# First products of seven stages by 512 columns, and five reorderings of read-outs and splits, in a two-block fp32 transformer kernel

## What is computed

```python
def first_block(x, mem, ...):
    for l in range(DEPTH):                       # DEPTH = 2, x is [1, 256, 1024]
        y = swiglu(rms_norm(x, ffn1_pre_g[l]), gate[l], up[l], down[l])   # 1024 -> 2816 -> 1024
        x = x + 0.5 * rms_norm(y, ffn1_post_g[l])
        y = hybrid_mixer(rms_norm(x, mix_pre_g[l]), w_in[l], ...)         # sparse attention and retention
        x = x + rms_norm(y, mix_post_g[l])
        y = memory_xattn(rms_norm(x, xa_pre_g[l]), rms_norm(mem, xa_mem_g[l]), wq, wk, wv, wo)
        x = x + rms_norm(y, xa_post_g[l])
        y = swiglu(rms_norm(x, ffn2_pre_g[l]), ...)
        x = x + 0.5 * rms_norm(y, ffn2_post_g[l])
    return x

def second_block(x, positions, ...):
    for l in range(DEPTH):
        h = rms_norm_2(x, g_pre_mix[l])
        u_pool, q, k, v, iq, ik, iw = jnp.split(h @ w_in[l], SPLIT_POINTS, axis=-1)
        ...                                      # rope, pooling mixer, top-k indexed attention
        x = x + rms_norm_2(jnp.concatenate([a_out, b_out], axis=-1) @ w_out[l], g_post_mix[l])
        h = rms_norm_2(x, g_pre_ffn[l])
        f = jnp.square(jax.nn.relu(h @ w_ff1[l])) @ w_ff2[l]              # 1024 -> 4096 -> 1024
        x = x + rms_norm_2(f, g_post_ffn[l])
    return x
```

## Time and profile before

| What | us |
|---|---|
| median of 3 runs | 1851.01 |
| lowest and highest | 1851.01, 1852.39 |
| the profiled execution | 1852.51 |
| its span, first to last instruction | 1850.7 |
| PE busy | 1830.4 (99%) |
| weight loads (PEld) busy | 1603.1 (87%) |
| DVE busy | 1315.3 (71%) |
| ACT busy | 1044.9 (56%) |
| POOL busy | 216.3 (12%) |
| mean granted TensorE clock | 0.999 of full |

### The profile page before, as it was taken

The page is one execution under the profiler, slowest core; times in us unless marked ns, Lnnn a source line. Parts: engine busy times, 40 slices in busy tenths (PEclk is TensorE's granted clock), DMA queues, the critical chain, the costliest instruction groups (busy, mean ns, idle before and its releaser), DMA issues.

```text
span 1850.7 us, 27918 instructions
## 1 busy us (share of the span) xinstructions
PE 1830.4 (99%) x10929; PEld 1603.1 (87%) x10929; DVE 1315.3 (71%) x1734; ACT 1044.9 (56%) x1503; POOL 216.3 (12%) x263
## 2 busy tenths in 40 slices
PE   8999999999999999999999999999999999999998
PEld 7888898898888888889988988888888888888887
DVE  6766758776766776676687677666887667787665
ACT  5655545665655565555566565556765445665543
POOL 1010102010100011001021000002101111301110
PEclk9999999999999999999999999999999999999999
DMA  9686654264665567766344446555446555635562
GB/s 316 195 293 194 176 175 137 92 204 149 205 205 182 182 204 229 246 171 225 126 137 163 145 157 218 195 184 172 175 137 215 195 182 166 228 123 185 184 201 71
DMA packets 229988, 339.48 MB, mean 183 GB/s; under 512 B 22294, under 2 KB 178080, under 8 KB 229856
## 3 DMA queue, kind: packets, MB, share of 16 engines
q1 hardware_dynamic: 222128, 308.43, 51.2%
q0 software_dynamic: 7728, 29.26, 4.7%
HBM read 336.62 MB, written 1.05 MB: 182 GB/s over the span
## 4 chain that ended last, share of the span: by engine, by line
PE 91%; DVE 5%; ACT 2%; issue 1%; DMA 0%; DVEq 0%; SPq 0%; ACTq 0%
PE ps L1702 88%; PE ps L1707 3%; DVE wlo L1111 2%; DVE region L1119 1%; ACT region L696 1%; DVE sm L1127 0%; ACT whi L696 0%; DMA raw<-ffn_w_gate 0%; DVE xn L1111 0%; DVE mlo L1111 0%; DVE ahl L1111 0%; DVE sm L1115 0%; DVE xs L1119 0%; DVE hlo L1111 0%; ACT ahl L696 0%
## 5 line engine op out<-in xcount | busy, mean ns | idle before, releaser
L1111 DVE TENSOR_TENSOR wlo<-raw,whi 128x1024 fp32r<-128x1024 f32 (+2 forms) x458 | 560.0, 1223 | 173.9 <-ACT whi L696 137.9
L696 ACT ACTIVATE whi<-raw 128x1024 fp32r<-128x1024 f32 (+2 forms) x458 | 483.4, 1055 | 62.5 <-PE ps L1702 16.2
L1702 PE MATMUL ps<-ahl,whi 128*128 128x512 f32 (+1 forms) x1920 | 433.4, 353 | 0.3
L1702 PEld LDWEIGHTS ps<-ahl,whi 128*128 128x128 f32 x1920 | 331.2, 190 | 43.1 <-DVE hlo L1111 0.9
L696 ACT ACTIVATE region<-ps 128x512 f32<-128x512 f32 (+2 forms) x260 | 150.6, 579 | 325.3 <-PE ps L1702 247.4
L1702 PE MATMUL ps<-whi,ahl 128*128 128x512 f32 (+2 forms) x1120 | 301.6, 347 | 1.8 <-DVE ahl L1111 1.4
L1702 PE MATMUL ps<-ahl,wlo 128*128 128x256 f32 x1568 | 269.0, 282 | 0.0
L1702 PEld LDWEIGHTS ps<-ahl,wlo 128*128 128x128 f32 x1568 | 233.3, 191 | 11.9
L1702 PEld LDWEIGHTS ps<-whi,ahl 128*128 128x128 f32 x1120 | 196.2, 189 | 27.8 <-DVE ahl L1111 3.4
L1111 DVE TENSOR_TENSOR mlo<-raw,mhi 128x1024 fp32r<-128x1024 f32 x130 | 160.8, 1237 | 48.8 <-ACT mhi L696 39.6
L1702 PE MATMUL ps<-wlo,ahl 128*128 128x512 f32 (+2 forms) x560 | 190.6, 340 | 0.0
(11 more groups left out here) (168 smaller groups left out, 2384.1 us busy)
## 6 DMA issues: line engine op xcount, KB each, us to landing
raw<-w_ff SPq DMA_DIRECT2D x64, 1024.0 KB, 5.4
raw<-ffn_w_up SPq DMA_DIRECT2D x44, 1024.0 KB, 5.8
raw<-ffn_w_down SPq DMA_DIRECT2D x44, 1024.0 KB, 5.0
raw<-ffn_w_gate SPq DMA_DIRECT2D x43, 1024.0 KB, 5.4
raw<-w_in SPq DMA_DIRECT2D x38, 1024.0 KB, 5.8
raw<-w_out SPq DMA_DIRECT2D x16, 1024.0 KB, 4.9
raw<-xa_wk SPq DMA_DIRECT2D x8, 1024.0 KB, 5.3
raw<-xa_wv SPq DMA_DIRECT2D x8, 1024.0 KB, 5.1
```

The costliest lines, as they stand in the source:

```text
L696: e.activation(o, i, f, **kw).then_inc(*act.did(*names))
L1111: e.tensor_tensor(o, a, b, op).then_inc(*dve.did(*names))
L1702: m = e.matmul(o, l, r, start=start, stop=stop)
```

## The change

- `weight_items`, `load`, `FIRST`, `BY_K`, `turn` and `begin` of PE: the first two items of an ffn stage are now called `front` and hold four blocks of rows of `gate` 0 and `up` 0 side by side (two DMAs each); the first two of relu and memory stages hold four blocks of rows by 512 columns. Every first product is 512 wide (or 584). The tokens of the second tile are transposed before part 6 of 8 and before the second tile, the scales before its part 7, in all stages.
- `begin`: fewer fillers, ACT and DVE turn the first activations before they split the first weights, item 1 is split in one go.
- relu: at the end of the first product DVE's split of the next item is taken half by half, one after each row tile.
- hybrid, ACT: in unit 1 the split of `wk` 3 goes ahead of the exponentials; in unit 5 the copy of memory piece 11 goes ahead of them.
- hybrid, DVE: `value(u - 1)` goes ahead of `head(u + 1)` and of the copy.
- sparse, ACT: the split of (`q`, 1) goes between the read-outs of the two row tiles.

The diff, cut to its core:

```diff
@@ -157,17 +157,20 @@
     def item(s, tag, src, k, n):
-        c = sum(1 for x in out if x[0][:2] == (s, tag))
+        c = sum(1 for x in out if x[0][:2] == (s, tag)) + (1 if tag in ("gate", "up") else 0)
         out.append(((s, tag, c), src, k, n))
...
             g, u, d = A[f + "_w_gate"][l, :, :], A[f + "_w_up"][l, :, :], A[f + "_w_down"][l, :, :]
-            for j in range(12):
+
+            for c in range(2):
+                item(s, "front", (rows(g, 4 * c, 4 * c + 4, 0, 256), rows(u, 4 * c, 4 * c + 4, 0, 256)), 4, 512)
+            for j in range(1, 12):
                 if j < 11:
...
                     item(s, "up", rows(u, 0, 8, 256 * j, 256 * j + 256), 8, 256)
-                if 1 <= j < 10:
+                if j < 10:
                     item(s, "down", rows(d, 2 * j - 2, 2 * j, 0, 1024), 2, 1024)
@@ -195,7 +198,9 @@
         elif kind == "memory":
-            for c in range(4):
+            for c in range(2):
+                item(s, "wq", rows(A["xa_wq"][l, :, :], 4 * c, 4 * c + 4, 0, 512), 4, 512)
+            for c in range(2, 4):
                 item(s, "wq", rows(A["xa_wq"][l, :, :], 0, 8, 256 * c, 256 * c + 256), 8, 256)
@@ -210,11 +215,12 @@
             f1, f2 = A["w_ff1_2"][l, :, :], A["w_ff2_2"][l, :, :]
-            for j in range(18):
+            for c in range(2):
+                item(s, "ff1", rows(f1, 4 * c, 4 * c + 4, 0, 512), 4, 512)
+            for j in range(2, 18):
                 if j < 16:
                     item(s, "ff1", rows(f1, 0, 8, 256 * j, 256 * j + 256), 8, 256)
-                if j >= 2:
-                    item(s, "ff2", rows(f2, 2 * j - 4, 2 * j - 2, 0, 1024), 2, 1024)
+                item(s, "ff2", rows(f2, 2 * j - 4, 2 * j - 2, 0, 1024), 2, 1024)
     return out
@@ -484,9 +490,8 @@
-        FIRST = {"ffn": (("gate", 0), ("up", 0)), "relu": (("ff1", 0), ("ff1", 1)), "hybrid": (("v_r", 0), ("v_r", 1)),
+        FIRST = {"ffn": (("front", 0), ("front", 1)), "relu": (("ff1", 0), ("ff1", 1)), "hybrid": (("v_r", 0), ("v_r", 1)),
                  "memory": (("wq", 0), ("wq", 1)), "sparse": (("index", 0), ("index", 1), ("index", 2))}
-        BY_K = {"ffn": False, "relu": False, "hybrid": True, "memory": False, "sparse": True}
@@ -499,6 +504,10 @@
                     q.wait_ge(*dve.at("lo", i - NRAW))
+                if tag == "front":
+                    for f in range(2):
+                        e.dma_start(dst[:, :, 256 * f:256 * f + 256], src[f]).then_inc(*raw_in[i % NRAW].did(("raw", i)))
+                    return
                 if tag != "q_n":
@@ -515,9 +524,11 @@
-            dst, src = raw_of(0).rearrange("p (k n) -> p k n", k=8), items[0][1]
-            e.dma_start(dst[:, 0:4, :], src[:, 0:4, :]).then_inc(*half_in.did(("raw", 0)))
-            e.dma_start(dst[:, 4:8, :], src[:, 4:8, :]).then_inc(*raw_in[0].did(("raw", 0)))
+            dst, src = raw_of(0).rearrange("p (k n) -> p k n", k=4), items[0][1]
+            for f in range(2):
+                e.dma_start(dst[:, 0:2, 256 * f:256 * f + 256], src[f][:, 0:2, :]).then_inc(*half_in.did(("raw", 0)))
+            for f in range(2):
+                e.dma_start(dst[:, 2:4, 256 * f:256 * f + 256], src[f][:, 2:4, :]).then_inc(*raw_in[0].did(("raw", 0)))
             x_half(1)
@@ -742,15 +753,13 @@
                 i0, i1 = first_items(0)
-                split_to(i0, halves=1)
                 halves(0, 0, 0, 0)
...
                 halves(0, 1, 0, 2)
-                split_to(i1, halves=1)
+                split_to(i1)
                 halves(0, 1, 1, 3)
-                split_to(i1)
                 row_square(0, 1)
@@ -947,17 +956,21 @@
                     put(hPT[u % 2][:, 0:512], PS[:, 0, :], ACT.Copy, ("h_pt", l, u))
-                    if u in (2, 3, 4, 5, 7):
+                    if u in (1, 2, 3, 4, 5, 7):
                         take(s, *HSPLIT[u], 0)
+                    if u == 5:
+
+                        memory_piece(s, 11)
                     if u < 7:
                         exps("h", l, u + 1, 128 * (HUNITS[u + 1][0] + 1), hP, 0.125)
-                    memory_piece(s, 2 * u + 1)
+                    if u != 5:
+                        memory_piece(s, 2 * u + 1)
                     if u == 2:
...
                         fin(s, l, 0)
-                    if u in (0, 1, 6):
+                    if u in (0, 6):
                         take(s, *HSPLIT[u], 0)
@@ -1050,6 +1063,8 @@
                     put(iqk[:, m, 292:576], PS[:, 4 + m, 0:284], ACT.Copy, ("iq_rest", l, m), scale=r2[:, m:m + 1])
+                    if m == 0:
+                        split_to(number[s, "q", 1])
                 for m in range(2):
@@ -1208,18 +1223,17 @@
                     weighted(0, 0, h)
+                halves(0, 0, 0, 0)
                 split_to(i0, halves=1)
-                halves(0, 0, 0, 0)
                 q.wait_ge(*x_in[1].at("x", 1))
...
                 weighted(0, 1, 1)
-                split_to(i1, halves=1)
+                split_to(i1)
                 halves(0, 1, 1, 3)
                 mean_square(0, 0)
-                split_to(i1)
                 mean_square(0, 1)
@@ -1281,7 +1295,7 @@
                         tt(HN[:, m, :], G[:, m, :], G[:, m, :], ALU.mult, ("hn", s, m))
-                        split_to(first_items(s)[-1] + 2)
+                        split_to(first_items(s)[-1] + 2, halves=1 + m)
                     else:
@@ -1506,13 +1520,13 @@
                 for u, (m, g, br) in enumerate(HUNITS):
+                    if u:
+                        value(u - 1)
                     if u < 7:
...
                         cp(hPT[u % 2][:, 512:1024], PS[:, 1, :], ("h_pt", l, u))
-                    if u:
-                        value(u - 1)
                     if u == 0:
@@ -1744,29 +1758,31 @@
                 it = first_items(0)
-                awake(6)
+                awake(2)
                 turn_tokens(0, 0, 0)
+                awake(2)
                 turn_tokens(0, 0, 1)
-                awake(12)
+                awake(9)
                 for i, n in enumerate(it):
...
                         ms = slice(m * 128, (m + 1) * 128)
-                        for k in range(8):
-                            if (i, m, k) == (0, 0, 4):
+                        for kk in range(4):
+                            if (i, m, kk) == (0, 0, 2):
                                 turn_tokens(0, 1, 0)
-                            if (i, m, k) == (0, 1, 0):
+                            if (i, m, kk) == (0, 1, 2):
                                 turn_tokens(0, 1, 1)
-                            if (i, m, k) == (1, 1, 7):
+                            if (i, m, kk) == (1, 1, 3):
                                 turn_scales(0)
-                            q.wait_ge(*dve.at("lo_half" if k < 4 else "lo", n))
-                            q.wait_ge(*dve.at("a", 0, m, k // 4))
-                            names = [("used", n)] if (m, k) == (1, 7) else []
-                            names += [("first", 0, m)] if (i, k) == (1, 7) else []
-                            three(PS[:, m, i * 256:(i + 1) * 256], ahv[:, k, ms], alv[:, k, ms], hi[:, k, :], lo[:, k, :], k == 0, k == 7, *names)
+                            q.wait_ge(*dve.at("lo_half" if kk < 2 else "lo", n))
+                            q.wait_ge(*dve.at("a", 0, m, i))
+                            names = [("used", n)] if (m, kk) == (1, 3) else []
+                            names += [("first", 0, m)] if (i, kk) == (1, 3) else []
+                            k = 4 * i + kk
+                            three(PS[:, m, :], ahv[:, k, ms], alv[:, k, ms], hi[:, kk, :], lo[:, kk, :], k == 0, k == 7, *names)
             def turn(s):
-                it, by_k = first_items(s), BY_K[kind_of(s)]
+                it = first_items(s)
@@ -1779,27 +1795,22 @@
                         else:
-                            outs = [(PS[:, m, 0:w] if by_k else PS[:, m, i * 256:(i + 1) * 256], slice(0, w))]
+                            outs = [(PS[:, m, 0:w], slice(0, w))]
                         hi, lo = weights(n)
-                        k = x if by_k else kk
-                        q.wait_ge(*dve.at("a", s, m, k // 4))
+                        q.wait_ge(*dve.at("a", s, m, x // 4))
                         ms = slice(m * 128, (m + 1) * 128)
...
                                 names += [("first", s, m)] if n == it[-1] else []
-                            three(o, ahv[:, k, ms], alv[:, k, ms], hi[:, kk, c], lo[:, kk, c], k == 0, k == 7, *names)
-
-                count = len(parts)
+                            three(o, ahv[:, x, ms], alv[:, x, ms], hi[:, kk, c], lo[:, kk, c], x == 0, x == 7, *names)
+
...
                 if kind_of(s) != "sparse":
-                    ahead[1][count - 1] = lambda: turn_scales(s)
-                ahead[0][count * 3 // 4 if by_k else 11] = lambda: turn_tokens(s, 1, 0)
-                if by_k:
-                    ahead[1][0] = lambda: turn_tokens(s, 1, 1)
-                else:
```

(4 more changed lines are left out.)

## The result

The changed kernel takes 1841.52 us (median of 6 runs, 1841.06 to 1841.71), the kernel before, run beside it, 1852.41 (6 runs, 1851.01 to 1852.54). The ratio is 0.9943, 95% interval 0.9930 to 0.9956: faster by 10.9 us of medians, and by 9.5 against those runs of before in which the clock did not fall (1851.0). The profiled execution took 1841.54 us, its span is 1839.5.

A forecast was written before the change was run, and what follows sets the result against it. PE-bound (TensorE busy 99%), so only less matmul time or fewer holes win; 2.65 + 1.0 + 1.6 + 3.0 + 0.5 = 8.8 us off 1851.0 gave 1842.2 us, range 1837.0 to 1847.0.

The forecast's parts named there:

- The reference point: The median of 1851.01 us was taken as a run without the clock's fall, priced at 1.6 us.
- Turns and j=1: Wide first products of seven later stages: 2.65 us; the wait in j=1's second product in four ffn stages: 1.0 us.
- The relu half split: Relu stages, half split on DVE: nothing gained, since no hole stands there.
- The start: Kernel start: first matmul at 11.4, second item's matmuls ending near 24.2 against 25.80, gaining 1.6 us, bounds 0.7 and 2.3.
- Hybrid: Stages s=1 and s=5: reordering gains 1.5 us a layer, 3.0 in all, limited by the chain to unit 7's transposes.
- the upper bound: Hybrid stages: at most 6.1 us, if the three holes of 1.27, 0.32 and 1.48 close whole.
- Sparse: Stages s=8 and s=10: the wait for DVE's split of (q, 1) goes, 0.5 us for both, bounds 0 and 0.5.
- (a): Hybrid gives nothing: PE stands as long at unit 7 or in w_out, DVE the real limit; 1845.2 us, chance 0.15.
- (b): Hybrid's holes close whole and the start reaches its bound, 3.1 and 0.7 us more; 1838.4 us, chance 0.16.
- (c): First products: wide matmuls cost as much as two narrow ones, 3.5 us lost; 1845.7 us, chance 0.05.
- (d): Only the width pays, 2.5 us, and the reordering gives nothing; 1848.5 us, chance 0.07.
- (e): Slower through the clock, at the start or turns: a first product at 1.2 GHz costs about 11 us; chance 0.05.

The follow-up runs named there:

- the filled hole: Kernel before with twelve useless identity transposes put into PE's hole of 1.45 us in hybrid unit 6, ahead of memory piece 12; 1850.81 us.
- the width alone: Kernel after with the hybrid, sparse and relu reorderings and the order of first splits and fillers undone, leaving the 512-column first products; 1848.81 us.
- all but the copy: Kernel before with value ahead of head on DVE and wk 3 split ahead of the exponentials on ACT, memory piece 11 not moved; 1849.36 us.
- the copy alone: Kernel before with only ACT's copy of memory piece 11 moved ahead of the exponentials in hybrid unit 5; 1850.77 us.
- the swap at unit 7: Kernel after with ACT's copy of the turned first tile (high half) ahead of the split of w_out 0 in hybrid unit 6; 1838.81 us.
- the relu edit undone: Kernel after with DVE again splitting both halves of the next weight item between its two squares in the relu stages; 1843.64 us.
- ACT's edits alone: Kernel before with ACT's split of wk 3 (unit 1) and copy of memory piece 11 (unit 5) ahead of the exponentials; 1850.03 us.
- all three in before: Kernel before with value ahead of head, wk 3 split and memory piece 11 copy ahead of the exponentials, nothing else; 1847.90 us.

## Why the prediction was right

The forecast was 1842.2 and the time 1841.52. Step by step:

- **The reference point.** That the median of 1851.01 is a run without the fall holds: the filled hole gives 1850.81. The price, 1.6 us from the distance between the layers, was measured as 1.58. What the reading of one profile missed: s=5's hole "had no such fall" there, but it can have one in other executions.
- **Turns and j=1.** Predicted 0.33 a turn with its wait and 0.25 for j=1; measured 0.32 and 0.37 in the memory stages and 0.68 in s=3 and s=4. s=7 missed its 0.25: there DVE stood 0.46 us between two of its own gating multiplies, so the low half of hidden 0 came no earlier. The relu stages gave 0.63 and 0.60 for 0.50: about 0.51 by the turn, and 0.1 at the hidden rows' transposes, the half split's. In the working for j=1, three wide matmuls are 0.69 us and not 0.77; the scales came 0.34 us earlier relative to PE, not 0.4, which was still enough for the wait of 0.25.
- **The relu half split.** The step "nothing; no hole stands there" failed. The hole is not in the trace of before because PE is not yet early enough; its cover was 0.06 us (square ended at 1395.36, transposes at 1395.42), and the turn's own gain of 0.51 used it up. That the total holds is luck in this term: the edit was part of the change, so the 2.1 us that are lost without it never had to be priced.
- **The start.** Predicted first matmul 11.4 and first product's end at 24.2; measured 11.61 and 24.32, against 25.80 before, so 1.48 for 1.6, and 0.35 for 0.25 around the wait in j=1. The waits between fell elsewhere than worked out (0.25 at 13.74, 0.37 at 15.33), the sum held. But the kernel without the reordering has the same gain; the order that I walked through step by step adds nothing that shows above the scatter of starts.
- **Hybrid.** Predicted 1.5 a layer, the next limit being the transposes of unit 7 with a wait of 0.8 us; measured 1.68 and 0.82. The chain written out from the earlier trace rows is the one that ACT's rows above show. The difference is the start of the chain: DVE's copy of unit 5 came at 344.29 for 347.80, 1.68 us earlier net of the 1.83 of the start, and not 1.45, since the hole of 0.32 at unit 4, which I left in the upper bound, closed too (0.37 us). But the copy's 1.45 us, which the working counted among the 2.8 that PE comes earlier, are no part of the 1.68: without the copy the net is 1.65. The term was right because it was taken from the chain, not from the holes.
- **Sparse.** Predicted 0.25 a stage; measured 0.48 and 0.35. The edit alone gives 0.37 and 0.38: 0.26 for the wait and 0.11 for a next step that is slow after a wait, which the working left out.

Of the rivals, (a) is what the copy alone does; (b) is what the swap at unit 7 comes near to, with 3.36 + 2.40 = 5.8 us for the hybrid of its 6.1, which shows that DVE's load was not the limit; (c) is excluded by 0.228 us a wide matmul, and (d) since the width alone takes 1848.81, 7.3 us more than the whole change; (e) did not occur: between its start and its last microseconds the profiled execution of the changed kernel never shows the lower level, and the other five have mean clocks of 0.999 or 1.0, where runs of before with one fall have 0.998.

**Open.** The stall of DVE of 0.46 us in s=7 stands, at the same instruction, in five profiles (after, the relu edit undone, ACT's edits alone, all three in before, all but the copy), with a loss of 0.3 us behind it. It is missing in the other nine, among them the kernel with the swap at unit 7, which has DVE's very order of the kernel after. The profile names no releaser but DVE itself, and the cause is open. Timeline of DVE after:

```profile
1093.79 0.42 DVE L1134 SCALAR_TENSOR_TENSOR region<-region,ps 128x256 f32<-128x256 f32 x1 [0.46 <-DVE region L1134]
```

## What to carry to other kernels

A hole that closes moves the engine forward only as far as the next chain allows (closing 1.45 us gave 0.1), so write that chain out with its engines, and look on it for an order that can be swapped: one swap on ACT gave 1.2 us a layer where the profile named DVE. An edit with no hole beside it can still be what keeps another edit's gain; ask of each place by how much its producer is early, and compare that with what the change brings. When runs fall into groups, look at the clock's rows first: one hole of 1.45 us cost 1.6 us more behind it, though filling it gave nothing else.

## What the runs showed of the hardware

- TensorE's granted clock fell to 1.2 GHz within a microsecond after a hole of 1.45 us, with PE in steady work ahead of it, in s=1 or in s=5, in about half of the executions, and by their times and mean clocks (0.997, groups 1.5 and 3.5 us above the lowest) twice in some, which no profile caught. Filled with twelve transposes, the hole brought no fall in ten runs. The holes of 1.25 to 1.29 us in unit 2 of six kernels had none behind them in any profile.
- A matmul of 512 columns (with its own weight load, fp32r) takes 0.228 us from start to start, one of 256 takes 0.1198. If the rest of the time goes by columns, that leaves about 0.012 us of fixed cost on each, an estimate from these two rows.
- A stall of 0.46 us between two DVE instructions, with no releaser on another engine, was there in the kernel after and gone when only the order on ACT in another stage was changed; why is open.
